# Another order of work between the down product and the output gate of a two-block transformer layer

## The chip, the cores and the metric

The kernel runs on one core of one Trainium2 chip. Its time is the device time of one execution in microseconds. The profile comes from one profiled execution; in it, TensorE (PE) does the matmuls and transposes, ScalarE (ACT), VectorE (DVE) and GpSimd (POOL) do the rest, and SyncE (SP) starts the DMA transfers of the weights.

## The reference

Two blocks run one after the other on x of 512 rows and 1024 columns, all in fp32. The first is a mixed attention layer, the second an attention and convolution layer with a feed-forward part and, at the very end, an input gate. What the change touches is the end of the second block:

```python
f = (jax.nn.silu(h @ w_gate[i]) * (h @ w_up[i])) @ w_down[i]   # down product, 2816 -> 1024
x = x + rmsnorm(f, ffn_post_norm[i])
e = rmsnorm(p[i] @ w_ple_proj[i], ple_norm[i])
x = x + jax.nn.sigmoid(x @ w_ple_gate[i]) * e                  # the gate, 1024 -> 1024
```

`rmsnorm(x, g)` is x / sqrt(mean(x^2) + 1e-6) * g over a row.

## The kernel before

**Precision.** Every operand of a product is kept as a high half and a low half (what the high half leaves over), and every product is three matmuls: high x high, high x low, low x high. Weights come in 142 chunks of 128 x 1024 through two raw buffers; ScalarE or GpSimd makes a chunk's high half (`w_hi`), GpSimd its low half (`w_lo`, two instructions of 128 x 512). There are four slots for split chunks, chunk c in slot c mod 4, and a slot is free again when the last matmul on its chunk has counted up `w_used`. For the down product ScalarE makes the high halves of the weights; for the gate GpSimd makes both.

**Rows.** The 512 rows stand in T = 4 row tiles of 128, called rows 0 to 3 here. The activations of the down product (`act`, 22 tiles of 128 x 512, k = 0..21) are staged one by one: ScalarE copies the high half into `aT_hi` (`stage` at line 1547), VectorE takes the low half (`stage` at line 2105), and TensorE waits for `staged`.

**The down product** (lines 1078 to 1122). `down_step(t, k)` is the six matmuls of row t with chunk k (two halves of 512 columns, three matmuls each). Up to k = 18 each chunk is used for all four rows (`down_block`, 24 matmuls); the last three chunks are used row by row, so that row 0 ends first. Row t fills PSUM banks 2t and 2t+1.

**What follows a row of it.** ScalarE squares the two banks with a row sum, VectorE adds the two sums (line 2134) and makes the mean (1636), ScalarE does logarithm and exponential (1205, 1206), VectorE three small Newton steps (1643 to 1648), then two scaled products (1631) and the addition to x (2009, counts up `x_new`). TensorE turns the new row of x with eight transposes into two tiles called xT (`turn_x`), ScalarE copies the high halves (`turned_hi`), VectorE takes the low halves (`turned_lo`, line 1663). `x_row(t)` is TensorE's wait for row t's halves.

**The gate** (lines 1125 to 1178). `pgate_step(g, t, n)` is the six matmuls of row t with chunk n of column half g; four chunks make a half. The first half runs mostly row by row, with the turns of rows 1 to 3 between: each turn has one to three steps of an earlier row behind it, before that row's halves are waited for. The second half takes chunks 0 and 1 for all rows, then chunks 2 and 3 row by row; its last row tile is done in two pieces of 256 columns. Sigmoid, product with `emb`, addition and store follow for each finished tile (lines 1607 to 1611 and 2143 to 2148).

**Order.** Every engine's instructions are written out by hand and run in that order; between engines there are only semaphores. `psum_tiles` (line 71) lists the PSUM tiles in the order in which they take their banks, each with the engine that empties it; from it come the counts that TensorE waits for.

## Time and profile before

| | |
|---|---|
| time, median of 3 runs | 946.56 us (944.69 to 948.07) |
| profiled execution | 944.69 us |
| its span on the core | 943.0 us |
| TensorE busy | 926.2 us (98%) |
| VectorE busy | 392.5 us (42%) |
| ScalarE busy | 331.2 us (35%) |
| GpSimd busy | 474.1 us (50%) |
| mean granted clock of TensorE | 0.994 |

The span runs from the first to the last instruction of the core; the profiled execution's own time is 1.7 us longer. The stage that the change touches is about the last 80 us: the block of k = 18 runs from 867 us, the rows of the down product after it to about 889 us, the first half of the gate to 916 us, the second to 939 us. In a stream, a matmul's duration is longer than the distance to the next one's start, since they are pipelined: the distances are what counts.

### The profile page before, as it was taken

What the parts mean: (1) busy time and instruction counts of PE and PEld (TensorE: products, weight loads), DVE (VectorE), ACT (ScalarE), POOL (GpSimd) and SP (SyncE); (2) the same over time, 40 slices, a digit from 0 to 9 for tenths busy, and PEclk for the clock granted to TensorE, in tenths of its full rate; (3) what the DMA queues carried; (4) which work ended last, traced back from release to release, by engine and by line L of the source; (5) the groups of instructions that cost most, each with busy time, mean ns of one, the idle gap of its engine ahead of it and who ended that gap; (6) DMA issues with size and microseconds to landing.
All of it is one profiled execution on the core that took longest, in us unless ns stands there. A gap on an engine that the chain in (4) does not pass through costs nothing.

```text
span 943.0 us, 12707 instructions
## 1 busy us (share of the span) xinstructions
PE 926.2 (98%) x4548; PEld 748.7 (79%) x4548; DVE 392.5 (42%) x647; ACT 331.2 (35%) x661; POOL 474.1 (50%) x376
## 2 busy tenths in 40 slices
PE   8999999999999999999999999999999999999998
PEld 7889877665578988886767988888888888888787
DVE  1654454557413283595648551111111122222662
ACT  3333414455312402175645842222222232323321
POOL 7967673230046776780334474454454445555543
PEclk9999999998999999999999999999999999999999
DMA  6432321100012332221111332322322322322213
GB/s 216 130 109 91 112 91 67 45 24 23 1 37 96 96 112 93 104 90 46 45 45 46 112 112 89 111 89 91 110 89 91 132 89 90 111 90 89 68 64 115
DMA packets 28058, 81.55 MB, mean 86 GB/s; under 512 B 5984, under 2 KB 8416, under 8 KB 28016
## 3 DMA queue, kind: packets, MB, share of 16 engines
q1 hardware_dynamic: 23856, 78.65, 25.1%
q10 hardware_dynamic: 4160, 2.32, 0.9%
q8 instruction: 29, 0.48, 0.2%
q14 instruction: 13, 0.11, 0.0%
HBM read 78.83 MB, written 2.10 MB: 86 GB/s over the span
## 4 chain that ended last, share of the span: by engine, by line
PE 90%; DVE 5%; issue 2%; POOL 1%; ACT 1%; DMA 1%; SPq 0%; DVEq 0%; POOLq 0%; ACTq 0%
PE bank L471 25%; PE bank L473 25%; PE bank L472 25%; PE bank L663 4%; PE bank L528 3%; PE bank L744 2%; PE bank L686 2%; PE bank L734 1%; PE bank L757 1%; POOL w_lo L429 1%; DVE aT_lo L1631 1%; DVE x L2009 1%; DMA raw<-in_weights 1%; DVE arena L1631 1%; DVE PT L1974 0%
## 5 line engine op out<-in xcount | busy, mean ns | idle before, releaser
L429 POOL TENSOR_TENSOR w_lo<-raw,w_hi 128x512 fp32r<-128x512 f32 x282 | 386.5, 1392 | 202.1 <-ACT w_hi L1199 196.1
L471 PE MATMUL bank<-w_hi,aT_hi 128*128 128x512 f32 (+4 forms) x600 | 227.3, 379 | 6.2 <-POOL w_lo L429 4.1
L471 PE MATMUL bank<-aT_hi,w_hi 128*128 128x512 f32 (+1 forms) x600 | 230.5, 384 | 0.0
L473 PE MATMUL bank<-aT_hi,w_lo 128*128 128x512 f32 (+1 forms) x600 | 227.1, 378 | 0.0
L472 PE MATMUL bank<-aT_lo,w_hi 128*128 128x512 f32 (+1 forms) x600 | 226.9, 378 | 0.0
L473 PE MATMUL bank<-w_hi,aT_lo 128*128 128x512 f32 (+4 forms) x600 | 222.1, 370 | 0.0
L472 PE MATMUL bank<-w_lo,aT_hi 128*128 128x512 f32 (+4 forms) x600 | 221.9, 370 | 0.0
L422 POOL TENSOR_SCALAR w_hi<-raw 128x1024 fp32r<-128x1024 f32 x73 | 80.6, 1104 | 246.8 <-PE bank L473 213.1
L1199 ACT ACTIVATE w_hi<-raw 128x1024 fp32r<-128x1024 f32 x68 | 72.1, 1062 | 233.4 <-PE bank L473 220.6
L471 PEld LDWEIGHTS bank<-w_hi,aT_hi 128*128 128x128 f32 x600 | 113.0, 188 | 26.1 <-POOL w_lo L429 6.7
L473 PEld LDWEIGHTS bank<-aT_hi,w_lo 128*128 128x128 f32 x600 | 112.9, 188 | 21.0
L471 PEld LDWEIGHTS bank<-aT_hi,w_hi 128*128 128x128 f32 x600 | 113.0, 188 | 20.0 <-issue 0.5
L472 PEld LDWEIGHTS bank<-aT_lo,w_hi 128*128 128x128 f32 x600 | 113.1, 188 | 19.8 <-issue 0.2
L473 PEld LDWEIGHTS bank<-w_hi,aT_lo 128*128 128x128 f32 x600 | 112.9, 188 | 19.1
L472 PEld LDWEIGHTS bank<-w_lo,aT_hi 128*128 128x128 f32 x600 | 113.1, 189 | 16.6
L2107 DVE TENSOR_TENSOR aT_lo<-arena,aT_hi 128x512 fp32r<-128x512 f32 x22 | 27.3, 1249 | 78.0 <-ACT aT_hi L1199 78.0
L2096 DVE TENSOR_TENSOR arena<-arena,bank 128x512 f32 (+1 forms) x22 | 15.1, 687 | 94.6 <-PE bank L473 93.7
L2093 DVE TENSOR_TENSOR arena<-bank,R 128x512 f32<-128x512 f32 x22 | 15.2, 691 | 89.3 <-PE bank L473 89.2
L1331 ACT ACTIVATE h<-bank,negmax 128x128 f32<-128x128 f32 (+1 forms) x64 | 33.8, 529 | 49.1 <-DVE negmax L1796 48.7
L1796 DVE TENSOR_REDUCE negmax<-bank 128x1 f32<-128x128 f32 (+1 forms) x64 | 31.2, 489 | 40.7 <-PE bank L665 39.4
L663 PE MATMUL bank<-arena 66*128 66x128 f32 (+7 forms) x128 | 45.7, 438 | 0.8 <-DVE arena L1695 0.8
L1199 ACT ACTIVATE arena<-bank,stat 128x512 f32<-128x512 f32 (+3 forms) x32 | 19.6, 612 | 44.5 <-PE bank L473 40.9
(202 smaller groups left out, 850.9 us busy)
## 6 DMA issues: line engine op xcount, KB each, us to landing
raw<-in_weights SPq DMA_DIRECT2D x142, 512.0 KB, 3.3
x<-in_x SPq DMA_DIRECT2D x4, 512.0 KB, 7.6
y_out<-x SPq DMA_DIRECT2D x7, 256.0 KB, 4.1
g_post<-in_gains ACTq DMA_DIRECT2D x3, 512.0 KB, 3.3
arena<-in_pt ACTq DMA_DIRECT2D x1, 512.0 KB, 3.8
y_out<-x SPq DMA_DIRECT2D x2, 128.0 KB, 1.9
wpool<-in_wpool ACTq DMA_DIRECT2D x1, 128.0 KB, 5.7
g_col<-in_gains ACTq DMA_DIRECT2D x3, 4.0 KB, 4.3
```

The source lines that it names most:

```text
L422: nc.gpsimd.tensor_scalar(w_hi[:, s, :], raw[:, r, :], 1.0, 1.0, ALU.mult, ALU.mult).then_inc(hi_made, 1)
L429: lo = nc.gpsimd.tensor_tensor(w_lo[:, s, at], raw[:, r, at], w_hi[:, s, at].bitcast(F32), ALU.subtract)
L471: mm(out, st_hi, mv_hi, start=start, stop=False)
L472: mm(out, st_hi, mv_lo, start=False, stop=False)
L473: return mm(out, st_lo, mv_hi, start=False, stop=stop)
L528: return nc.tensor.transpose(out, in_, ident[:, :])
L663: mm(out[:, 0:kw], qT_[0:width, i, qb * P:(qb + 1) * P], kT_[0:width, i, 0:kw], start=True, stop=False)
L686: last = mm(bank[6][r0:r0 + HD, kb * P:S], v_[:, kb, i * HD:(i + 1) * HD], pt_of[i % 3][:, kb, kb * P:S], start=(kb == 0), stop=(kb == T - 1),
L1199: return A(out, in_, ACT.Copy, scale=scale)
L1331: A(P_buf[:, n % 4, 0:kw], bank[n % 3][:, 0:kw], ACT.Exp, bias=negmax[:, n % 8:n % 8 + 1], accum_out=esum[:, n % 8:n % 8 + 1]).then_inc(ex ...
L1796: V.tensor_reduce(negmax[:, n % 8:n % 8 + 1], bank[n % 3][:, 0:kw], AX_X, ALU.max, negate=True)\
L2107: V.tensor_tensor(aT_lo[:, slot, :].unsqueeze(1), act[:, bass.ds(k, 1), :], aT_hi[:, slot, :].bitcast(F32).unsqueeze(1), ALU.subtract).the ...
```

## The change

It rewrites the order of this last stage on four engines; no matmul is added or dropped.

- TensorE: the last four chunks of the down product, not three, are used row by row. Row 0 is turned after row 2 of the down product, row 1 inside row 3 ahead of its last two chunks, row 2 behind row 3. Then gate chunks 0 and 1 run for rows 0 to 2; then row 3 is turned and does chunks 0 and 1; then chunks 2 and 3 run for all rows. The second half of the gate runs row by row over all four chunks.
- ScalarE: in the down product, the copy of activation k comes just ahead of the weights of chunk k+3, no longer one further ahead; the last three copies (k = 19, 20, 21) all stand behind the last weights (chunk 21). The high halves of rows 0 and 1 stand ahead of row 3's squares, those of rows 2 and 3 behind row 3's square root.
- VectorE: the low halves of rows 0 and 1 stand ahead of row 3's sum, row 2's ahead of row 3's scaled products; none stands between scaled products and addition any more. The release of a down tile's banks counts after the addition.
- The table of PSUM tiles follows the new order: turned tiles 0 to 3 take banks 0 to 3, the others banks 4 to 7.

```diff
@@ psum_tiles
     for t in range(T):
-        if t == T - 1:
-            for n in range(2):
+        for g in range(2):
+            tiles["down", t, g] = (2 * t + g, "dve" if t < T - 1 else "dve_last",
+                                   CH["down"] + NF - 1 if (t, g) == (T - 1, 1) else None)
+        if t == T - 2:
+            for n in range(4):
                 tiles["xT", n] = (n, "dve", None)
...
@@ tensor
-            for k in range(4 * rounds, NF - 3):
+            for k in range(4 * rounds, NF - 4):
                 down_block(k, k % 4)
...
             for t in range(T):
-                if t == T - 1:
-                    turn_x(range(1))
-                for k in range(NF - 3, NF):
+                for k in range(NF - 4, NF):
                     if t == 0:
                         pe.wait_ge(staged, k + 1)
                         pe.wait_ge(w_split, k + CH["down"] + 1)
+                    if t == T - 1 and k == NF - 2:
+                        turn_x(range(1, 2))
                     down_step(t, k % 4, end=(k == NF - 1))
+                if t == T - 2:
+                    turn_x(range(0, 1))
...
-            def gate_row(t, ns):
-                for n in ns:
+            turn_x(range(2, T - 1))
+            for n in range(2):
+                for t in range(T - 1):
+                    if n == 0:
+                        x_row(t)
+                    pgate_step(0, t, n)
+            turn_x(range(T - 1, T))
+            x_row(T - 1)
+            for n in range(2):
+                pgate_step(0, T - 1, n).then_inc(w_used, 1)
+            for n in range(2, 4):
+                for t in range(T):
                     last = pgate_step(0, t, n)
                     if t == T - 1:
                         last.then_inc(w_used, 1)
                     elif n == 3:
                         last.then_inc(tile_full, 1)
-
-            x_row(0)
-            gate_row(0, (0,))
-            turn_x(range(1, 2))
-            gate_row(0, (1, 2))
-            x_row(1)
-            gate_row(1, (0, 1))
-            turn_x(range(2, 3))
-            gate_row(0, (3,))
-            gate_row(1, (2, 3))
-            x_row(2)
-            gate_row(2, (0,))
-            turn_x(range(3, 4))
-            gate_row(2, (1, 2, 3))
-            x_row(T - 1)
-            gate_row(T - 1, range(4))
-
-            halves = ((slice(0, S // 2), ("pgate", 1, T - 1)), (slice(S // 2, S), ("pgate", 2, T - 1)))
-            for n in range(2):
-                for t in range(T - 1):
-                    pgate_step(1, t, n)
-                pgate_step(1, T - 1, n, *halves[0])
-                pgate_step(1, T - 1, n, *halves[1]).then_inc(w_used, 1)
...
+            for n in range(3):
+                pgate_step(1, 0, n)
+            pgate_step(1, 0, 3).then_inc(tile_full, 1)
+            for t in range(1, T - 1):
+                for n in range(4):
+                    last = pgate_step(1, t, n)
+                last.then_inc(tile_full, 1)
+            for n in range(4):
+                last = pgate_step(1, T - 1, n, slice(0, S // 2))
+            last.then_inc(tile_full, 1)
+            for n in range(4):
+                pgate_step(1, T - 1, n, slice(S // 2, S), ("pgate", 2, T - 1)).then_inc(w_used, 1)
@@ scalar
-            stage(4, 0, CH["down"] + 1)
             rounds = (NF - 4) // 4
             with act_.Fori(1, rounds) as i:
                 for j in range(4):
-                    stage(i * 4 + (j + 1), (j + 1) % 4, i * 4 + (CH["down"] + j - 2))
+                    stage(i * 4 + j, j, i * 4 + (CH["down"] + j - 3))
                     down_weights(i * 4 + j, j)
             for k in range(4 * rounds, NF - 3):
-                stage(k + 1, (k + 1) % 4, CH["down"] + k - 2)
-                if k == NF - 4:
-                    stage(k + 2, (k + 2) % 4, CH["down"] + k - 1)
+                stage(k, k % 4, CH["down"] + k - 3)
                 down_weights(k, k % 4)
-            stage(NF - 1, (NF - 1) % 4, CH["down"] + NF - 4)
+            for k in range(NF - 3, NF):
+                stage(k, k % 4, CH["down"] + k - 3)
...
             for t in range(T):
-                if t == T - 2:
-                    turned_hi("xT", range(1))
+                if t == T - 1:
+                    turned_hi("xT", range(0, 2))
                 for g in range(2):
                     full(act_, ("down", t, g))
                     squares(tbank(("down", t, g))[:, :], 16 + 2 * t + g, stat[:, 3, 12 + t:13 + t])
-                if t == T - 1:
-                    turned_hi("xT", range(1, 2))
                 rsqrt(slice(24 + t, 25 + t))
@@ vector
             for t in range(T):
+                if t == T - 1:
+                    turned_lo("xT", range(0, 2))
                 sqn[0] += 2
                 dve.wait_ge(sq_done, sqn[0])
...
                 newton(24 + t, stat[:, 3, 12 + t:13 + t])
-                add_post(t, [(g * 512, (g + 1) * 512, tbank(("down", t, g))[:, :]) for g in range(2)], 24 + t,
-                         lambda: down_read(t))
+                if t == T - 1:
+                    turned_lo("xT", range(2, T - 1))
+                add_post(t, [(g * 512, (g + 1) * 512, tbank(("down", t, g))[:, :]) for g in range(2)], 24 + t)
+                for g in range(2):
+                    if t < T - 1:
+                        order[0] += 1
+                    V.sem_inc(drained[tiles["down", t, g][3][0]], 1)
```

The numbers of lines in the rows below are each kernel's own; those of the changed kernel are 2 to 14 lower for the same statement.

ScalarE at the end of the down product, before: the copies `aT_hi<-arena` are activations 17; 18; 19 and 20; 21, and the `w_hi<-raw` between them are chunks 19, 20 and 21.

```order
L1199 ACTIVATE aT_hi<-arena 128x512 [waits w_used]
L1199 ACTIVATE w_hi<-raw 128x1024 [waits w_used,raw_in1]
L1199 ACTIVATE aT_hi<-arena 128x512 [waits w_used]
L1199 ACTIVATE w_hi<-raw 128x1024 [waits w_used,raw_in0]
L1199 ACTIVATE aT_hi<-arena 128x512 [waits w_used] x2
L1199 ACTIVATE w_hi<-raw 128x1024 [waits w_used,raw_in1]
L1199 ACTIVATE aT_hi<-arena 128x512 [waits w_used]
```

The same place in the changed kernel; the copies are activations 16; 17; 18; then 19, 20 and 21.

```order
L1191 ACTIVATE aT_hi<-arena 128x512 [waits w_used]
L1191 ACTIVATE w_hi<-raw 128x1024 [waits w_used,raw_in1]
L1191 ACTIVATE aT_hi<-arena 128x512 [waits w_used]
L1191 ACTIVATE w_hi<-raw 128x1024 [waits w_used,raw_in0]
L1191 ACTIVATE aT_hi<-arena 128x512 [waits w_used]
L1191 ACTIVATE w_hi<-raw 128x1024 [waits w_used,raw_in1]
L1191 ACTIVATE aT_hi<-arena 128x512 [waits w_used] x3
```

Activations 19 and 20 moved from ahead of the last weights to behind them.

TensorE at the turn of row 3 (`ident,x` are its transposes), before:

```order
L528 MATMUL bank<-ident,x 128x128 [waits drained_dve_last,x_new]
L528 MATMUL bank<-ident,x 128x128 x3
L528 MATMUL bank<-ident,x 128x128 [waits drained_dve_last]
L528 MATMUL bank<-ident,x 128x128 x3
L471 MATMUL bank<-w_hi,aT_hi 128x512 [waits w_split]
```

And in the changed kernel:

```order
L526 MATMUL bank<-ident,x 128x128 [waits drained_dve_last,x_new]
L526 MATMUL bank<-ident,x 128x128 x3
L526 MATMUL bank<-ident,x 128x128 [waits drained_dve_last]
L526 MATMUL bank<-ident,x 128x128 x3
L469 MATMUL bank<-w_hi,aT_hi 128x512 [waits drained_dve,w_split,mix_lo]
```

The matmul behind the turn was one of row 2, which waits for a chunk alone; now it is row 3's own first, which waits for the low halves (`mix_lo`).

VectorE from row 3's sum on, in the changed kernel; the four low halves ahead of the sum are those of rows 0 and 1, the two behind the Newton steps those of row 2:

```order
L1651 TENSOR_TENSOR aT_lo<-bank,aT_hi 128x4x128 [waits mix_hi]
L1651 TENSOR_TENSOR aT_lo<-bank,aT_hi 128x4x128 [waits mix_lo,mix_hi] x3
L2116 TENSOR_TENSOR stat<-stat 128x1 [waits mix_lo,sq_done]
L1624 TENSOR_SCALAR stat<-stat 128x1 [waits dve_step]
L1631 TENSOR_SCALAR stat<-stat 128x1 [waits rs_made]
L1632 TENSOR_SCALAR stat<-stat 128x1 [waits dve_step]
L1636 TENSOR_SCALAR stat<-stat 128x1 [waits dve_step]
L1651 TENSOR_TENSOR aT_lo<-bank,aT_hi 128x4x128 [waits mix_hi,dve_step]
L1651 TENSOR_TENSOR aT_lo<-bank,aT_hi 128x4x128 [waits mix_lo,mix_hi]
L1619 SCALAR_TENSOR_TENSOR PT<-bank,stat,g_post 128x512 [waits mix_lo]
```

Before, row 3's sum came straight after the addition of row 2, and row 2's low halves between row 3's scaled products and its addition.

```order
L2009 TENSOR_TENSOR x<-x,PT 128x1024 [waits mix_lo]
L2134 TENSOR_TENSOR stat<-stat 128x1 [waits sq_done]
L1636 TENSOR_SCALAR stat<-stat 128x1 [waits dve_step]
L1643 TENSOR_SCALAR stat<-stat 128x1 [waits rs_made]
L1644 TENSOR_SCALAR stat<-stat 128x1 [waits dve_step]
L1648 TENSOR_SCALAR stat<-stat 128x1 [waits dve_step]
L1631 SCALAR_TENSOR_TENSOR PT<-bank,stat,g_post 128x512 [waits dve_step] x2
L1663 TENSOR_TENSOR aT_lo<-bank,aT_hi 128x4x128 [waits dve_step,mix_hi]
L1663 TENSOR_TENSOR aT_lo<-bank,aT_hi 128x4x128 [waits mix_lo,mix_hi]
L2009 TENSOR_TENSOR x<-x,PT 128x1024 [waits mix_lo]
```

So row 2's low halves moved ahead of the scaled products, and those of rows 0 and 1 came to stand between row 2's addition and row 3's sum.

## Rows read from the trace of the kernel before

**Rows 1.** The page: TensorE's share of the span; the chain by engine.
```profile
PE 926.2 (98%) x4548; PEld 748.7 (79%) x4548; DVE 392.5 (42%) x647; ACT 331.2 (35%) x661; POOL 474.1 (50%) x376
...
PE 90%; DVE 5%; issue 2%; POOL 1%; ACT 1%; DMA 1%; SPq 0%; DVEq 0%; POOLq 0%; ACTq 0%
```

**Rows 2.** Waits of TensorE, 600 us to the end: sum, times, longest.
```profile
PE bank L471 <- POOL w_lo L429: 2.3, 2, 2.0
```

**Rows 3.** TensorE by time: start, duration (us), line, operation, count, idle before.
```profile
866.99 0.39 PE L471 MATMUL bank<-w_hi,aT_hi 128*128 128x512 f32 x1
...
868.35 0.39 PE L471 MATMUL bank<-w_hi,aT_hi 128*128 128x512 f32 x1
...
893.10 0.39 PE L473 MATMUL bank<-w_hi,aT_lo 128*128 128x512 f32 x1
895.44 0.50 PE L471 MATMUL bank<-w_hi,aT_hi 128*128 128x512 f32 x1 [1.95 <-POOL w_lo L429]
...
905.99 1.03 PE L528 MATMUL bank<-ident,x 128*128 128x128 f32 x8
906.78 0.47 PE L471 MATMUL bank<-w_hi,aT_hi 128*128 128x512 f32 x1
...
916.19 0.39 PE L473 MATMUL bank<-w_hi,aT_lo 128*128 128x512 f32 x1
916.91 0.50 PE L471 MATMUL bank<-w_hi,aT_hi 128*128 128x512 f32 x1 [0.33 <-POOL w_lo L429]
...
939.07 0.28 PE L473 MATMUL bank<-w_hi,aT_lo 128*128 128x256 f32 x1
```

**Rows 4.** ScalarE by time, last weights' and last activations' high halves.
```profile
867.25 1.06 ACT L1199 ACTIVATE w_hi<-raw 128x1024 fp32r<-128x1024 f32 x1 [3.34 <-PE bank L473]
868.21 0.61 ACT L1199 ACTIVATE aT_hi<-arena 128x512 fp32r<-128x512 f32 x1
```

**Rows 5.** VectorE by time, low halves of the activations.
```profile
863.53 2.96 DVE L2107 TENSOR_TENSOR aT_lo<-arena,aT_hi 128x512 fp32r<-128x512 f32 x2 [4.18 <-ACT aT_hi L1199]
868.86 1.37 DVE L2107 TENSOR_TENSOR aT_lo<-arena,aT_hi 128x512 fp32r<-128x512 f32 x1 [2.37 <-ACT aT_hi L1199]
```

**Rows 6.** GpSimd by time, high and low halves of gate chunks 0 and 4.
```profile
872.78 1.05 POOL L422 TENSOR_SCALAR w_hi<-raw 128x1024 fp32r<-128x1024 f32 x1 [1.40 <-issue]
873.91 2.53 POOL L429 TENSOR_TENSOR w_lo<-raw,w_hi 128x512 fp32r<-128x512 f32 x2
...
912.68 1.24 POOL L422 TENSOR_SCALAR w_hi<-raw 128x1024 fp32r<-128x1024 f32 x1 [12.70 <-PE bank L473]
914.01 2.85 POOL L429 TENSOR_TENSOR w_lo<-raw,w_hi 128x512 fp32r<-128x512 f32 x2
```

**Rows 7.** VectorE by time, row 0's sum, last Newton step, addition to x.
```profile
877.78 0.16 DVE L2134 TENSOR_TENSOR stat<-stat 128x1 f32<-128x1 f32 x1 [7.55 <-ACT PT L1213]
...
879.34 0.27 DVE L1648 TENSOR_SCALAR stat<-stat 128x1 f32<-128x1 f32 x1
...
881.43 1.23 DVE L2009 TENSOR_TENSOR x<-x,PT 128x1024 f32<-128x1024 f32 x1 [0.25 <-DVE PT L1631]
```

**Rows 8.** VectorE by time, row 1's addition, row 2's sum, row 3's low halves.
```profile
887.69 1.70 DVE L2009 TENSOR_TENSOR x<-x,PT 128x1024 f32<-128x1024 f32 x1
889.31 1.25 DVE L2134 TENSOR_TENSOR stat<-stat 128x1 f32<-128x1 f32 x1
...
907.26 1.53 DVE L1663 TENSOR_TENSOR aT_lo<-bank,aT_hi 128x512 fp32r<-128x512 f32 x2 [2.32 <-ACT aT_hi L1199]
```

**Rows 9.** ScalarE by time, row 3's high halves and the last sigmoid.
```profile
906.63 1.09 ACT L1199 ACTIVATE aT_hi<-bank 128x512 fp32r<-128x512 f32 x2 [5.25 <-PE bank L528]
...
939.38 0.38 ACT L1611 ACTIVATE PT<-bank 128x256 f32<-128x256 f32 x1 [1.05 <-DVE x L2148]
```

**Rows 10.** Windows: busy us of PE, PEld, DVE, ACT, POOL; granted clock, DMA share, GB/s.
```profile
220.00:225.00 5.00, 5.00 (x11) 2.51 (x11) 4.92 (x9) 2.73 (x6) 0.00 (x0) 0.50 0.00 0
...
892.00:900.00 8.00, 6.05 (x29) 4.66 (x29) 6.78 (x11) 2.14 (x6) 7.74 (x6) 1.00 0.39 131
```

More of the change, by code:

```diff
@@ L152, in psum_tiles @@
     for t in range(T):
-        if t == T - 1:
-            for n in range(2):
+        for g in range(2):
[3 more added lines that the diff above has]
+            for n in range(4):
                 tiles["xT", n] = (n, "dve", None)
-        for g in range(2):
-            tiles["down", t, g] = (2 * t + g, "dve_last", CH["down"] + NF - 1 if (t, g) == (T - 1, 1) else None)
-    for n in range(2, 6):
+    for n in range(4, 2 * T):
         tiles["xT", n] = (n, "dve", None)
     for t in range(T):
-        if t == 2:
-            for n in range(6, 2 * T):
-                tiles["xT", n] = (n, "dve", None)
         tiles["pgate", 0, t] = (t, "act", CH["pgate"] + 3 if t == T - 1 else None)
@@ L1148, in gate_row @@
                         last.then_inc(tile_full, 1)
-            x_row(0)
-            gate_row(0, (0,))
-            turn_x(range(1, 2))
-            gate_row(0, (1, 2))
-            x_row(1)
-            gate_row(1, (0, 1))
-            turn_x(range(2, 3))
-            gate_row(0, (3,))
-            gate_row(1, (2, 3))
-            x_row(2)
-            gate_row(2, (0,))
-            turn_x(range(3, 4))
-            gate_row(2, (1, 2, 3))
-            x_row(T - 1)
-            gate_row(T - 1, range(4))
-            halves = ((slice(0, S // 2), ("pgate", 1, T - 1)), (slice(S // 2, S), ("pgate", 2, T - 1)))
-            for n in range(2):
-                for t in range(T - 1):
-                    pgate_step(1, t, n)
-                pgate_step(1, T - 1, n, *halves[0])
-                pgate_step(1, T - 1, n, *halves[1]).then_inc(w_used, 1)
-            for t in range(T - 1):
-                pgate_step(1, t, 2)
-                pgate_step(1, t, 3).then_inc(tile_full, 1)
-            pgate_step(1, T - 1, 2, *halves[0])
-            pgate_step(1, T - 1, 3, *halves[0]).then_inc(tile_full, 1)
-            for n in (2, 3):
-                pgate_step(1, T - 1, n, *halves[1]).then_inc(w_used, 1)
+            for n in range(3):
[10 more added lines that the diff above has]
+                pgate_step(1, T - 1, n, slice(S // 2, S), ("pgate", 2, T - 1)).then_inc(w_used, 1)
         @block.scalar
@@ L1999, in _, with add_post @@
             V.sem_inc(sqs_made, 1)
-            def add_post(t, halves, at, between=None):
+            def add_post(t, halves, at):
                 for n, (lo_c, hi_c, value) in enumerate(halves):
@@ L2005, in add_post @@
                     own(stt(w, value, stat[:, 3, at:at + 1], g_post[:, lo_c:hi_c], ALU.mult, ALU.mult))
-                if between:
-                    between()
                 xn[0] += 1
@@ L2124, in _ @@
             dve.wait_ge(g_post_in, 48)
-            def down_read(t):
-                for g in range(2):
-                    V.sem_inc(drained["dve_last"], 1)
-                if t > 0:
-                    turned_lo("xT", range(t - 1, t))
             for t in range(T):
+                if t == T - 1:
+                    turned_lo("xT", range(0, 2))
                 sqn[0] += 2
```

## Prediction

> **What bounds the kernel now.** I read the page's busy shares and its chain by engine first. TensorE is busy for 926.2 of 943.0 us, and 90% of the chain that ended last is TensorE [rows 1]. So the time is TensorE's fixed work plus its pauses. The diff touches only the last 80 us or so. There I went to the waits of that window, then to TensorE's instructions in order of time, then to ScalarE, VectorE and GpSimd beside them.
>
> Between 860 us and the end TensorE pauses twice, both times for a low half made by GpSimd, 2.3 us in all [rows 2]. In a steady stream a 512-column matmul starts 0.227 us after the one before (the rows at 866.99 and 868.35 are six apart) [rows 3]. Counted from start to start, the first pause is 895.44 - 893.10 - 0.23 = 2.1 us and the second 916.91 - 916.19 - 0.23 = 0.5 us; the first matmul after a pause costs 0.1 more than the pitch, in every pause. This is the only time in the stage that another order could win back: **2.6 us**. The other waits of TensorE there are hidden by matmuls that stand between a turn and the row that needs it.
>
> **The change, part by part.** The matmuls are the same in number and size, and so are the four pairs of turned tiles. A step here is the six matmuls of one chunk for one row, 6 x 0.227 = 1.36 us; a row of the gate or of the down product over four chunks is four steps, 5.44 us; two turned tiles with the restart cost 906.78 - 905.99 + 0.1 = 0.9 us [rows 3]. What changes is who is ready when.
>
> **(a) Staging of the last four chunks of the activations.** The block of all rows for k=17 ends at 866.99, where before had another whole block (k=18) to run, to 866.99 + 24 x 0.227 = 872.43. Now row 0 of k=18..21 begins there, and k=19 is wanted after one step, at 868.35 [rows 3]. But ScalarE now copies the high half of k=19 only behind the weights of chunk 21, and these wait for the end of the block of k=17: in the trace they start at 867.25, and a copy behind them at 868.21 [rows 4]. VectorE's low half follows at 868.86; it took 1.37 alone and 2.96 for two in a row, about 1.48 each, beside GpSimd's splits [rows 5]. So k=19 is ready between 868.86 + 1.25 and + 1.48, about 870.3: a pause of 1.95 and 0.1 for the restart. k=20 and k=21 come 1.48 apart, against steps of 1.36: 0.1 to 0.2 more. **2.2 us**, bounds 1.9 and 2.4. In the loop before it the same delay is harmless: the low half is done 3 us into a block of 5.44. Row 0 then ends at 874.65, row 2 at 885.55, row 3 with both turns at 892.75.
>
> **(b) GpSimd and the gate's chunks.** Gate chunk 0 takes the slot of down chunk 18, which now is free only after row 3's first step, 887.8; GpSimd starts 0.3 later, as at 872.78 behind the block that ended at 872.43, and a chunk takes 3.6 (1.05 + 2.53) to 4.5 us [rows 6]. So chunk 0 is there at 891.8 to 893.1, chunk 1 at 895.5 to 897, chunks 2 and 3 by about 905. They are wanted at 893.6, about 900 and 910: no pause, and the 2.1 us of before go, because the order now does two chunks for three rows before it needs the third. The splits are only later, and that puts them beside VectorE's row chain, which counts in (c).
>
> **(c) Row 2 of the new order.** TensorE turns row 2 at 892.75, does step (row 0, chunk 0), (row 1, chunk 0), and wants row 2's halves at 892.75 + 0.9 + 2 x 1.36 = 896.4. VectorE's queue before these halves is: row 2's addition to x, four low halves of rows 0 and 1, row 3's sum of squares, its mean and Newton steps. The unhindered chain, from row 0 of before: the row ends at 876.5, the sum starts at 877.78, the Newton steps end at 879.61 = 1.83 later, the addition ends at 882.66, 6.15 after the row's end [rows 7]. So row 2 (end 885.55) has its new x at 891.7. The four low halves take 2 x 1.53 [rows 8]: VectorE is free at 894.9. The squares of row 3 are done at 892.75 + 1.27 = 894.0 and don't decide. From the sum on: 1.83 + 1.53 = 3.4. ScalarE's high halves of row 2, now behind row 3's square root, start with its end, 0.8 before the Newton steps do, and take 1.1 [rows 9]; they are hidden. Without any hindrance row 2 is ready at 898.3: a pause of 1.9 + 0.1.
>
> There is a hindrance. The sum took 0.16 us in the free chain, but 1.25 at 889.31, while GpSimd was making a low half, and the 128x1024 addition took 1.23 alone but 1.70 beside it [rows 7, 8]. In the changed kernel GpSimd splits chunk 0 and chunk 1 from 888.1 on, over this very addition and sum. If both are hit as in those rows, row 2 is ready 1.1 + 0.5 later, and with 0.3 more if the sum has to let a second low half through, a pause of 3.9; if VectorE is free as soon as the squares are (894.0) and nothing hits, 1.2. I take 2.7, one hit of two: **2.7 us**, bounds 1.2 and 3.9. The Trainium skill ("SBUF — State Buffer", section "SBUF: two separate sides") says that VectorE with two SBUF inputs and GpSimd exclude each other for a whole instruction. By that rule the pause would lie between 2.0 and 3.9, by how many of the two meet a split; without it, it would be 2.0. The trace agrees with it in the 1.25 against 0.16.
>
> **(d) Row 3 of the new order.** Row 3's turn and its first use now stand next to each other: three steps of row 2 stood between. From turn to low half in the trace: 905.99 to 907.26 + 1.53 = 908.79, with ScalarE and VectorE idle before [rows 3, 8, 9]. Of these 2.8 us the turn itself covers 0.8, and 0.1 is the switch that is paid anyway. Row 3's x is ready by about 903, before TensorE comes to turn it at 904.5. **2.1 us**, bounds 2.0 and 2.2 (TensorE's own rows give no other price for it).
>
> **(e) The second half of the gate.** Its first row now takes all four chunks in a row, and its chunk 3 sits in a slot that the very last step of the first half frees. That step is three steps, 4.1 us, ahead of the use. GpSimd started 912.68, 0.34 after such a step, and took 4.2 us beside VectorE's output products (2.85 + 1.24 + a gap), 3.7 without [rows 6]. So it is ready 4.0 to 5.0 after the step: 0 to 0.9, and since VectorE still has the first half's four outputs to do at that time, **0.5 us**. It stands where the 0.5 of before stood.
>
> **(f) The end.** The last half tile ends in product, addition and store as before. Before, the last sigmoid's row names VectorE's addition of the tile before as its releaser, which would be a gain now that this tile is done 2.9 us earlier; but it starts at 939.38, only 0.03 after the last matmul's end (939.07 + 0.28), so at most 0.03 is to be had [rows 3, 9]. Steps of down that gave up the turn before row 3 and took it back as two: 0. Later notice of the free down banks: VectorE's count now comes after the addition, but the turn waits for that addition anyway: 0.
>
> **The sum**: 2.2 + 2.7 + 2.1 + 0.5 - 2.6 = **+4.9 us**. On the profiled execution (944.69 us, of which 943.0 span and 1.7 around it) that is 949.6; this execution was the fastest of the three shown, 1.9 under their median, and a median of the changed kernel should stand to 946.56 as this stands to that: **951.5 us**. The bounds of all terms together are +2.5 and +6.8, that is 949.1 to 953.4.
>
> **The rivals.** About 0.3%, 2.8 us, is what a measurement of this kernel can tell from no change.
>
> - *VectorE has caught up (not slower by what can be told).* Place: row 2's halves. If the addition and the sum slip through between GpSimd's instructions, and row 3's squares decide, (c) is 1.2; if chunk 3 then is in time too, the sum is 2.2 + 1.2 + 2.1 - 2.6 = +2.9, and with (a) at 1.9, +2.6: 949.2. It decides from (c) below 1.1 with (e) at zero. For it: both instructions are short against GpSimd's gaps. Against it: GpSimd has no gap while two splits are pending. Chance 0.13, and 0.03 more that something I took for fixed gives time back and it is faster.
> - *The clock falls.* Three pauses of 2 to 3 us within 40 us are new. In this trace TensorE's granted clock is 1.00 from 892 to 900 us, around the 2.1 us pause, but between 220 and 225 us, with 11 matmuls in 5 us, it was 0.50, the lower of its two levels (1.2 of 2.4 GHz) [rows 10]. That stretch lost 5 x 0.5 = 2.5 us. The same here would give +7.4: 954.0. Against it: dense 512-column matmuls stand around each pause, and the clock held in the like case. Chance 0.07. The Trainium skill ("TensorE: Matmul & The Clock Gate", Part 1) has the half clock as the state an idle engine goes back to; this trace agrees only for the sparse stretch.
> - *The staging pause isn't there*, because the copies slip ahead somewhere I misread: +2.7, 949.3. ScalarE runs its queue in order and the waits are in its rows, so 0.04; it is part of the 0.13.
>
> **How the numbers follow.** The forecast, with (a) to (e) in their bounds and the clock at its full level, has 0.77; the clock 0.07; the catching up 0.13; faster 0.03. The forecast's low corner, below +2.8, is in the 0.13. So slower 0.84, same 0.13, faster 0.03. The range: the bounds 949.1 to 953.4, widened by about a microsecond below and one and a half above for medians of a kernel whose three runs spread over 3.4 us, and for the clock's case: 948.2 to 955.0.
>
> **What would show it.** In the changed trace: a pause of about 2 us in row 0 of the last down chunks, released by VectorE's low half of the activations (a); no pause for gate chunks 1 and 2 (b); a pause of 1.2 to 3.9 released by VectorE's low half of x about 4 us after the turn of row 2, and VectorE's sum ahead of it at over 1 us if the hindrance is real (c); a pause of 2.1 right behind the turn of row 3 (d); at most 0.9 for GpSimd three steps into the second half (e). I am wrong if (a) or (d) is missing, if a pause appears in the loop before 866 us, or if the clock leaves 1.00 there.

## The result and the profile after

The changed kernel took 951.05 us, the median of 13 executions (947.97 to 954.84), against 946.56 us before, also of 13. The medians differ by 4.5 us; the ratio on record, which is not simply the quotient of these medians, is 1.0054 with a 95% interval of 1.0039 to 1.007, that is 5.1 us more (3.7 to 6.6). The prediction was 951.5 us, and slower.

The two profiled executions are further apart than that, 951.42 us against 944.69, and part of this lies ahead of the change. ScalarE starts on the weights of chunk 21, 0.26 us behind the end of the block of k = 17, at 869.44 us instead of 867.25 [rows 4], 2.19 us later, though TensorE has no wait between 600 and 866 us in either trace. Most of it arose where TensorE's work is sparse: the same ScalarE instruction starts 0.31 us later in the changed kernel at about 208 us (208.75 against 208.44) and 2.16 us later at about 296 us (297.22 against 295.06). The windows from 200 to 300 us (columns as in [rows 10]), first of the kernel before, then of the changed kernel:

```profile
200.00:300.00 100.00, 98.36 (x417) 65.85 (x412) 41.48 (x85) 31.94 (x75) 22.22 (x19) 0.95 0.10 32
```

```profile
200.00:300.00 100.00, 98.36 (x406) 64.92 (x403) 40.93 (x84) 32.14 (x77) 22.11 (x18) 0.93 0.10 32
```

The granted clock was 0.95 of full speed in one and 0.93 in the other. So in what follows the **stage**, the stretch that the change touches, is measured by itself: from ScalarE's start on the weights of chunk 21 to the start of the last matmul. It was 939.07 - 867.25 = 71.82 us before and is 945.80 - 869.44 = 76.36 us after: **4.54 us more**, against +4.9 predicted.

TensorE's waits in the stage, as in [rows 2]: sum, times, longest.

```profile
PE bank L469 <- DVE aT_lo L1651: 3.5, 2, 1.8
PE bank L469 <- DVE aT_lo L2093: 1.7, 1, 1.7
PE bank L469 <- POOL w_lo L427: 0.8, 1, 0.8
```

Before there were two waits for GpSimd's low halves of weights, 2.3 us. Now there are three for VectorE, 5.2 us, and one for GpSimd. The same in TensorE's order of time (the answer to [rows 3]):

```profile
870.32 0.39 PE L471 MATMUL bank<-w_hi,aT_lo 128*128 128x512 f32 x1
872.45 0.51 PE L469 MATMUL bank<-w_hi,aT_hi 128*128 128x512 f32 x1 [1.74 <-DVE aT_lo L2093]
...
887.88 1.03 PE L526 MATMUL bank<-ident,x 128*128 128x128 f32 x8
...
895.12 1.03 PE L526 MATMUL bank<-ident,x 128*128 128x128 f32 x8
...
898.52 0.39 PE L471 MATMUL bank<-w_hi,aT_lo 128*128 128x512 f32 x1
900.63 0.50 PE L469 MATMUL bank<-w_hi,aT_hi 128*128 128x512 f32 x1 [1.72 <-DVE aT_lo L1651]
...
906.21 1.03 PE L526 MATMUL bank<-ident,x 128*128 128x128 f32 x8
...
909.06 0.50 PE L469 MATMUL bank<-w_hi,aT_hi 128*128 128x512 f32 x1 [1.81 <-DVE aT_lo L1651]
...
926.65 0.39 PE L471 MATMUL bank<-w_hi,aT_lo 128*128 128x512 f32 x1
927.80 0.50 PE L469 MATMUL bank<-w_hi,aT_hi 128*128 128x512 f32 x1 [0.76 <-POOL w_lo L427]
...
945.80 0.28 PE L471 MATMUL bank<-w_hi,aT_lo 128*128 128x256 f32 x1
```

The pause at 872.45 is row 0 waiting for activation k = 19, the one at 900.63 is row 2 of the gate, the one at 909.06 is row 3 right behind its turn (906.21), the one at 927.80 the last weight chunk of the second half. ScalarE and VectorE around the first (the answer to [rows 4, 5]):

```profile
869.44 1.06 ACT L1191 ACTIVATE w_hi<-raw 128x1024 fp32r<-128x1024 f32 x1 [3.86 <-PE bank L471]
870.41 1.65 ACT L1191 ACTIVATE aT_hi<-arena 128x512 fp32r<-128x512 f32 x3
```

```profile
871.16 3.53 DVE L2093 TENSOR_TENSOR aT_lo<-arena,aT_hi 128x512 fp32r<-128x512 f32 x3 [4.18 <-ACT aT_hi L1191]
...
892.31 1.67 DVE L1995 TENSOR_TENSOR x<-x,PT 128x1024 f32<-128x1024 f32 x1
893.90 3.19 DVE L1651 TENSOR_TENSOR aT_lo<-bank,aT_hi 128x512 fp32r<-128x512 f32 x4
897.24 0.31 DVE L2116 TENSOR_TENSOR stat<-stat 128x1 f32<-128x1 f32 x1
...
899.05 1.53 DVE L1651 TENSOR_TENSOR aT_lo<-bank,aT_hi 128x512 fp32r<-128x512 f32 x2
```

The copies of 19, 20 and 21 stand in one piece behind the weights, and VectorE's three low halves behind them. The other rows of VectorE are row 2's addition to x, the four low halves of rows 0 and 1, row 3's sum and row 2's low halves (the answer to [rows 7, 8]). GpSimd beside them (the answer to [rows 6]): high and low halves of gate chunk 0, then the low halves of chunk 1.

```profile
890.48 1.05 POOL L420 TENSOR_SCALAR w_hi<-raw 128x1024 fp32r<-128x1024 f32 x1 [16.94 <-issue]
891.61 3.53 POOL L427 TENSOR_TENSOR w_lo<-raw,w_hi 128x512 fp32r<-128x512 f32 x2
...
896.24 2.54 POOL L427 TENSOR_TENSOR w_lo<-raw,w_hi 128x512 fp32r<-128x512 f32 x2
```

### The profile page after: what moved, and what is told of

Read it like the earlier page. It is cut to its first block, busy times and chain, and to the rows that moved or that the text cites. A ratio compares the mean times of both kernels' runs of the same rounds, so it can differ in the third digit from the quotient of the medians.

```text
span 949.7 us, 12711 instructions
## 1 busy us (share of the span) xinstructions
PE 928.8 (98%) x4548; PEld 749.2 (79%) x4548; DVE 389.8 (41%) x647; ACT 331.4 (35%) x661; POOL 474.6 (50%) x376
## 4 chain that ended last, share of the span: by engine, by line
PE 90%; DVE 6%; ACT 1%; issue 1%; DMA 1%; POOL 1%; POOLq 0%; DVEq 0%; SPq 0%; ACTq 0%
PE bank L469 25%; PE bank L471 25%; PE bank L470 25%; PE bank L661 4%; PE bank L526 3%; PE bank L742 2%; PE bank L684 2%; PE bank L732 1%; PE bank L755 1%; DVE aT_lo L1619 1%; DVE x L1995 1%; DVE aT_lo L1651 1%; DVE PT L1619 1%; DMA raw<-in_weights 1%; DVE arena L1619 1%
```

## The experiments

Each was run beside the kernel before on the same chip; "stage" is the length defined above, in one profiled execution each.

| run | median, us (executions) | ratio to before, 95% interval | stage, us |
|---|---|---|---|
| kernel before, beside the changed kernel | 946.56 (13) | | 71.82 |
| changed kernel | 951.05 (13) | 1.0054 (1.0039 to 1.007) | 76.36 |
| e1, copies ahead | 949.09 (10) | 1.0046 (1.0029 to 1.0063) | 74.56 |
| e2, row 2 later | 948.5 (10) | 1.0042 (1.0021 to 1.0062) | 74.57 |
| e3, row 3 covered | 953.2 (5) | 1.009 (1.0056 to 1.0123) | 80.21 |
| e4, second half | 949.61 (10) | 1.005 (1.0032 to 1.0069) | 76.98 |
| e5, all four | 942.78 (12) | 0.998 (0.9966 to 0.9994) | 69.66 |
| e6, before with late copies | 944.19 (10) | 0.9985 (0.9969 to 1.0002) | 71.81 |
| e7, short low halves | 951.82 (1) | | 77.01 |
| e8, short splits | 949.36 (1) | | 74.73 |
| e9, changed again | 951.29 (4) | 1.0061 (1.0038 to 1.0083) | 78.25 |
| e10, changed a third time | 946.42 (1) | | 76.53 |
| e11, all four again | 944.41 (12) | 0.9984 (0.9968 to 1.0) | 69.63 |

The kernel before had medians of 945.05 beside e1 to e4, 945.28 beside e5 to e7 and 945.2 beside e8 to e11. The ratios are those on record and differ a little from the quotients of the medians (0.9974 for e5). The totals are too close together to part single terms of 1 to 2 us (the intervals are 2.6 us wide or more); the stage is what tells them apart.

### e1: the copies ahead again

```diff
+            stage(4, 0, CH["down"] + 1)
...
-                    stage(i * 4 + j, j, i * 4 + (CH["down"] + j - 3))
+                    stage(i * 4 + (j + 1), (j + 1) % 4, i * 4 + (CH["down"] + j - 2))
                     down_weights(i * 4 + j, j)
...
-            for k in range(NF - 3, NF):
-                stage(k, k % 4, CH["down"] + k - 3)
+            stage(NF - 1, (NF - 1) % 4, CH["down"] + NF - 4)
```

> The changed kernel with ScalarE's order of activation copies as in the kernel before (one further ahead, 19 and 20 ahead of the weights of chunk 21); all else as changed. Theory: late copies alone make the pause in row 0 of the last down chunks; it goes, and since everything behind it depends on row ends, nothing takes its place. The stage, from ScalarE's start on the weights of chunk 21 to the start of the last matmul, was 76.36 us in the changed kernel and 71.82 before; it should be 74.0, the total about 2.4 us (0.25%) under the changed kernel. Rival: the pause only hides that the row chain behind it is late, and a pause of like size comes back at row 1's or row 2's turn: stage 76.0 or more.

The stage fell by 1.80 us, and nothing came back at the later rows. But it did not fall by the whole 2.4, so it ended at 74.56 and not at the expected 74.0. TensorE in row 0, changed kernel with copies ahead:

```profile
872.54 0.39 PE L471 MATMUL bank<-w_hi,aT_lo 128*128 128x512 f32 x1
873.22 0.47 PE L469 MATMUL bank<-w_hi,aT_hi 128*128 128x512 f32 x1 [0.29 <-POOL w_lo L427]
```

The wait moved from k = 19 to k = 21, and its releaser from VectorE's activations to GpSimd's low half of the weights of chunk 21. These can't start before the block of k = 17 has ended, in either order. So of the 2.4 us, 1.8 belong to the late copies and 0.6 to starting row-by-row work one chunk earlier; of these 0.6, this wait is 873.22 - 872.54 - 0.23 = 0.45.

### e2: row 2 after four steps

```diff
-            for n in range(2):
-                for t in range(T - 1):
-                    if n == 0:
-                        x_row(t)
-                    pgate_step(0, t, n)
+            for t in range(2):
+                x_row(t)
+                pgate_step(0, t, 0)
+            for t in range(2):
+                pgate_step(0, t, 1)
+            x_row(2)
+            for n in range(2):
+                pgate_step(0, 2, n)
```

> The changed kernel with four steps instead of two between row 2's turn and row 2's first step: rows 0 and 1 do gate chunks 0 and 1 before row 2 starts. Theory: the pause of 1.9 us before row 2 is VectorE's queue (low halves of rows 0 and 1, row 3's statistics, then row 2's halves) against a cover of two steps; two more steps of 1.36 cover it. Gate chunk 1 is ready at about the time it is wanted. Stage 76.4 - 1.9 = 74.5. Rival: GpSimd's chunk 1 takes the place of the wait, as chunk 2 does in the kernel before: a pause of 0.5 to 2 for a low half of weights, stage 75 to 76.4.

The stage fell by 1.79, and TensorE's waits in it are those of the changed kernel less one:

```profile
PE bank L469 <- DVE aT_lo L1654: 1.8, 1, 1.8
PE bank L469 <- DVE aT_lo L2096: 1.7, 1, 1.7
PE bank L469 <- POOL w_lo L427: 0.7, 1, 0.7
```

The pause before row 2 is gone and chunk 1 did not take its place. The theory held.

### e3: two steps behind row 3's turn

```diff
             turn_x(range(T - 1, T))
+            for t in range(2):
+                pgate_step(0, t, 2)
             x_row(T - 1)
...
             for n in range(2, 4):
-                for t in range(T):
+                for t in range(2 if n == 2 else 0, T):
```

> The changed kernel with two steps (rows 0 and 1, gate chunk 2) between row 3's turn and row 3's first step. Theory: the 2.05 us behind row 3's turn are the bare way from turn to low half and any two steps cover them; chunk 2 is split 4 us earlier. Stage 76.4 - 2.05 = 74.3. Rival: chunk 2 isn't there, or the second half's chunks 4 and 5, whose slots row 3 frees two steps later than before, come late: stage 75 to 77.

The pause behind the turn went, as expected, and the stage still grew by 3.85 us. The rival is what happened, and more, though at other chunks than it named: chunks 6 and 7, not 4 and 5. GpSimd, the high halves of chunks 4 to 7 of the gate and the last low half:

```profile
909.49 1.05 POOL L420 TENSOR_SCALAR w_hi<-raw 128x1024 fp32r<-128x1024 f32 x1 [4.51 <-PE bank L471]
...
913.12 1.05 POOL L420 TENSOR_SCALAR w_hi<-raw 128x1024 fp32r<-128x1024 f32 x1
...
917.22 1.50 POOL L420 TENSOR_SCALAR w_hi<-raw 128x1024 fp32r<-128x1024 f32 x1
...
922.05 1.49 POOL L420 TENSOR_SCALAR w_hi<-raw 128x1024 fp32r<-128x1024 f32 x1
923.63 3.25 POOL L427 TENSOR_TENSOR w_lo<-raw,w_hi 128x512 fp32r<-128x512 f32 x2
```

All four splits of the second half now stand end to end; in the changed kernel the first three did, and the fourth began after a gap of 0.85 us (the row at 923.15 under (e) below). The first starts 5.3 us behind row 3's turn (909.49 - 904.15) instead of 4.7 (910.90 - 906.21), because row 3 frees chunk 0 two steps later, while the pause that is gone lets the second half begin 2.1 us sooner. TensorE waits first for chunk 6 (0.61 us idle before the matmul at 922.14), then for chunk 7, whose split ends at 926.88:

```profile
923.40 0.40 PE L471 MATMUL bank<-w_hi,aT_lo 128*128 128x512 f32 x1
926.93 0.79 PE L469 MATMUL bank<-w_hi,aT_hi 128*128 128x512 f32 x1 [3.13 <-POOL w_lo L427]
927.52 0.63 PE L470 MATMUL bank<-w_lo,aT_hi 128*128 128x512 f32 x1
927.95 0.63 PE L471 MATMUL bank<-w_hi,aT_lo 128*128 128x512 f32 x1
```

After 3.13 us of pause the matmuls come 0.43 us apart instead of 0.23: the granted clock was 0.57 from 925 to 930 us and 0.74 from 930 to 935. From this pause to the end took 947.58 - 926.93 = 20.65 us, against 945.80 - 927.80 = 18.00 us in the changed kernel for the same work. The pause cost 926.93 - 923.40 - 0.23 = 3.30 us and the clock another 2.65. Together: -2.06 for the pause that is gone, +0.76 for chunk 6, 3.30 - 0.92 = +2.38 for chunk 7 and +2.65 for the clock are +3.7, of 3.85 measured.

### e4: the second half in its old order

```diff
-            for n in range(3):
-                pgate_step(1, 0, n)
-            pgate_step(1, 0, 3).then_inc(tile_full, 1)
...
+            for n in range(2):
+                for t in range(T - 1):
+                    pgate_step(1, t, n)
+                pgate_step(1, T - 1, n, *halves[0])
+                pgate_step(1, T - 1, n, *halves[1]).then_inc(w_used, 1)
...
```

> The changed kernel with the second half of the gate in the order of the kernel before (chunks 0 and 1 for all rows, then 2 and 3 row by row); the first half as changed. Theory: the pause of 0.8 to 0.9 us three steps into the second half is the split of its last chunk; in this order that chunk is wanted 8 steps or more later, and the pause of 0.5 that the kernel before had at the start of its second half doesn't return, because the first half's order as changed frees slots 0 and 1 early. Stage 76.4 - 0.9 = 75.5. Rival: the pause only moves to another chunk: 76.4.

The pause went and did not move:

```profile
PE bank L469 <- DVE aT_lo L1652: 3.5, 2, 1.8
PE bank L469 <- DVE aT_lo L2094: 1.7, 1, 1.7
```

Yet the stage was 0.62 longer, not 0.9 shorter. Behind row 3's turn, in a stretch that this edit doesn't touch, TensorE ran

```profile
908.61 0.50 PE L469 MATMUL bank<-w_hi,aT_hi 128*128 128x512 f32 x1 [1.81 <-DVE aT_lo L1652]
...
909.98 0.63 PE L471 MATMUL bank<-w_hi,aT_lo 128*128 128x512 f32 x1
910.41 0.63 PE L469 MATMUL bank<-w_hi,aT_hi 128*128 128x512 f32 x1
```

at 0.43 us a matmul from 909.98 on, for 3.3 us. That is the lower level of the clock (granted 0.50 in the window from 910 to 913 us), behind a pause that is the same in the changed kernel (1.81 us idle). 76.98 less the expected 75.5 is 1.5 us. The expectation was wrong in total and right in the term it was made for; the clock is taken up in e9.

### e5 and e11: all four edits

The edits of e1 to e4 together, in one kernel.

> The changed kernel with all four edits at once (copies ahead, row 2 after four steps, two steps behind row 3's turn, second half in the order of before). Theory: the four pauses are independent, and with the two early pauses for weights gone that the change does remove, TensorE has no pause over 0.3 us left in the stage: 76.36 - 2.38 - 1.9 - 2.05 - 0.87 = 69.2 us, 2.6 under the kernel before, total about 0.27% faster than before. Rival: the pauses cover each other (VectorE and GpSimd used them to catch up), and a new one of 1 to 2 us appears at gate chunk 1 or 2: stage 70.5 to 71.5, no measurable gain on before.

The stage was 69.66 us, and TensorE's waits in it

```profile
PE bank L469 <- POOL w_lo L427: 0.3, 1, 0.3
```

are the 0.3 us for chunk 21 seen in e1. Counted from start to start this wait is 0.45, and 71.82 - 2.6 + 0.45 = 69.67. The expected 69.2 had missed it: it took off the whole 2.4 of row 0, where moving the copies wins back only 1.8. What failed by itself in e3 works here: the four splits stand end to end here too (they start at 904.29, 907.93, 912.03 and 916.87), but with the second half in the old order chunk 7 is wanted late enough. The total was 0.2% under the kernel before, 0.998 (0.9966 to 0.9994). A second time:

> The kernel with all four edits once more, for its interval against the kernel before. Theory: no pause over 0.3 us behind the down product, so no fall of the clock in the stage: stage 69.7, total 0.2% to 0.3% under the kernel before. Rival: the first gain was chance of the mean clock: no difference.

69.63 us, and 0.9984 (0.9968 to 1.0). The stage repeats to 0.03 us; 71.8 - 69.65 = 2.2 us, 0.23%, agrees with both ratios. The second interval reaches 1.0, so that the gain in total rests on the first and on the stage.

### e6: late copies in the kernel before

The kernel before with ScalarE's part of the change alone (the diff of e1 turned round).

> The kernel before with ScalarE's order of activation copies as changed (19, 20 and 21 behind the weights of chunk 21); all else as before. Theory: late copies cost only together with row-by-row work that starts at k=18; here a block of all four rows at k=18 (5.4 us) stands between and hides them: stage 71.8 as before, no difference in total. Rival: late copies cost by themselves, somewhere in the loop or at k=19: stage 73 to 74.

Stage 71.81 us, and the two waits of before, to a tenth:

```profile
PE bank L471 <- POOL w_lo L429: 2.3, 2, 2.0
```

Late copies cost nothing while a block of four rows stands between. They cost 1.8 us once row-by-row work begins a chunk earlier: neither edit is expensive alone.

### e7 and e8: GpSimd out of VectorE's way

```diff
-                    at = slice(half * 512, (half + 1) * 512)
+                    at = slice(half * 512, half * 512 + width)
...
+            for c in range(CH["pgate"], NCH):
+                split(c, c % SLOTS, False, skipped=CH["pgate"] - SHARED, width=32)
```

> The changed kernel with GpSimd's low halves of the eight gate chunks made for 32 of each 512 columns only, so that part of the low halves of the gate's weights is left out; it takes GpSimd's long instructions away from beside VectorE's row chain. Theory (VectorE with two operands in SBUF waits for GpSimd's instruction): row 2's addition falls from 1.67 to 1.23 us and row 3's sum from 0.31 to 0.16, the pause before row 2 from 1.9 to 1.3, and the pause for the last chunk of the second half goes (0.9): stage 76.4 - 0.6 - 0.9 = 74.9. Rival (GpSimd has no hand in the pause before row 2): that pause stays at 1.9, stage 75.5.

The pause before row 2 stayed at 1.9 us, which was the rival's number, but the run doesn't decide: row 2's addition was not set free. (The stage of 77.01 lacks the pause for the last chunk, as expected, and has instead the fall of the clock that e9 is about.) VectorE's addition and the GpSimd instruction that it now met, gate chunk 1's high half:

```profile
891.99 1.85 DVE L1996 TENSOR_TENSOR x<-x,PT 128x1024 f32<-128x1024 f32 x1
```

```profile
891.73 1.05 POOL L420 TENSOR_SCALAR w_hi<-raw 128x1024 fp32r<-128x1024 f32 x1
```

1.85 us, against 1.23 alone. So e8 leaves out most of the high halves of the gate's weights too:

```diff
-                    nc.gpsimd.tensor_scalar(w_hi[:, s, :], raw[:, r, :], 1.0, 1.0, ALU.mult,
+                    hw = slice(0, CW if width == 512 else 32)
+                    nc.gpsimd.tensor_scalar(w_hi[:, s, hw], raw[:, r, hw], 1.0, 1.0, ALU.mult,
```

> The changed kernel with both halves of the eight gate chunks made for 32 columns of 512 (low) and 32 of 1024 (high), so that most of the split of the gate's weights is left out and GpSimd is next to idle in the stage. With the low halves alone shortened, GpSimd's high half at 891.73 met row 2's addition instead (1.85 us), so the hindrance was not removed. Theory: now the addition takes 1.23, row 2's halves come 0.4 to 0.6 earlier against row 2's turn, and the pause before row 2 falls from 1.9 to 1.3 to 1.5. Rival: the addition is not what the low halves of rows 0 and 1 wait for, and the pause stays within 0.1 of 1.9.

VectorE's addition, the four low halves of rows 0 and 1 and row 3's sum, then TensorE at row 2:

```profile
891.80 1.23 DVE L1997 TENSOR_TENSOR x<-x,PT 128x1024 f32<-128x1024 f32 x1
892.94 3.20 DVE L1653 TENSOR_TENSOR aT_lo<-bank,aT_hi 128x512 fp32r<-128x512 f32 x4
896.29 0.16 DVE L2118 TENSOR_TENSOR stat<-stat 128x1 f32<-128x1 f32 x1
```

```profile
899.53 0.50 PE L471 MATMUL bank<-w_hi,aT_hi 128*128 128x512 f32 x1 [1.15 <-DVE aT_lo L1653]
```

The addition took 1.23 us and the sum 0.16. From row 2's turn (its place in the stage is 25.70) to row 2's first step (30.62) it took 4.92 us instead of 5.51: the pause is 1.3 instead of 1.9. The hindrance by GpSimd is worth 0.6 us (0.44 at the addition, 1.67 for 1.23, and 0.15 at the sum, 0.31 for 0.16); the rest of the pause is VectorE's queue itself. The addition and the sum have both operands in SBUF and were held up; the four low halves, with one operand in PSUM, took 3.19 us beside GpSimd's splits (893.90 in the changed kernel) and 3.20 without. Both agree with the rule of the Trainium skill ("SBUF — State Buffer", section "SBUF: two separate sides") that VectorE, when both its inputs are in SBUF, and a GpSimd instruction that reads SBUF exclude each other for a whole instruction.

### e9 and e10: the changed kernel again

> The changed kernel once more. Theory: its executions come in two kinds, by whether TensorE's granted clock falls to the lower level behind the pause at row 3's turn: stage 76.4 us without (as in the trace of the changed kernel), 77.9 with (as the two variants with the second half reordered and with short low halves showed). The times of all executions then follow the mean clock at about 900 us for each unit of it (0.9 us for 0.001). Rival: the fall belonged to those two variants alone, stage 76.4 always.

> The changed kernel a third time, for the same question: a stage of 76.4 us (clock 1.00 throughout) or of 77.9 (a fall behind the turn of row 3). If neither this nor the run before it shows 77.9, the fall is not shown for the changed kernel itself.

The stage was 78.25 us in e9 and 76.53 in e10, with the same pauses before and behind row 3's turn. The windows around the pause behind that turn, first e9 (pause until 907.24), then e10 (until 903.90):

```profile
905.00:910.00 5.00, 3.19 (x13) 2.39 (x12) 1.38 (x2) 2.37 (x3) 0.75 (x2) 0.83 0.34 108
910.00:915.00 5.00, 5.00 (x20) 4.02 (x19) 0.00 (x0) 0.00 (x0) 4.83 (x5) 0.83 0.13 32
```

```profile
900.00:905.00 5.00, 3.19 (x19) 2.53 (x18) 1.38 (x2) 2.37 (x3) 1.87 (x2) 1.00 0.34 107
905.00:910.00 5.00, 5.00 (x24) 4.14 (x23) 0.00 (x0) 0.00 (x0) 4.18 (x4) 1.00 0.01 3
```

0.83 twice against 1.00 twice: the same program, with and without the fall. The price can be read between two matmuls that are the same in all: from the restart behind the turn to the last matmul ahead of the next pause took 926.46 - 907.24 = 19.22 us in e9, against 17.58 in e10 and 926.65 - 909.06 = 17.59 in the first trace of the changed kernel, 1.6 us more. The rest of the 1.7 to 1.9 us between the stages is a longer wait for the last chunk (1.15 us in e9, 1.07 in e10, 0.92 in the first trace). Counting every trace with this pause behind the turn of row 3 (the changed kernel, e1, e2, e4, e7, e8, e9, e10), the clock fell there in three of eight: e4, e7, e9. It fell 1.0 to 1.4 us after the matmuls had begun again (in e4 they began at 908.61 and the pitch of 0.43 us at 909.98), not in the pause itself.

The expectation had a second part, and it was too simple: the mean clock of an execution orders the totals, but this is another matter than the fall behind the turn. The executions of the changed kernel run from 947.97 us at a mean clock of 0.996 to 954.84 at 0.989, 0.98 us for each 0.001, near the 0.9 expected. Yet the first trace and e9 took nearly the same time, 951.42 and 951.46 us, one without the fall and one with it: the windows from 200 to 300 us have a granted clock of 0.93 and 0.95 there, and of 0.98 in e10 with its 946.42 us. So in these two the sparse stretch far ahead of the change made up for the fall, and a total doesn't tell whether the fall was there. The spread of 3.4 us between the first three executions of before is of the size that such differences of the clock give.

## Why the prediction was right, point by point

Each pause that was forecast is there, at its place and with its releaser, and an edit aimed at each takes it away: e1 for (a), but for the 0.45 us of chunk 21, e2 for (c), e3 for (d), where others come in its place, and e4 for (e). That the number came out closer than its terms is luck: (a) is 0.2 too small, (e) 0.4 too small and (c) 0.8 too large.

| term | predicted, us (bounds) | measured, us | read from |
|---|---|---|---|
| early pauses gone | -2.6 | -2.6 | no wait for gate chunks 0 to 6 |
| (a) activation k = 19 | +2.2 (1.9 to 2.4) | +2.4 | 887.88 - 869.18 - 72 x 0.2267 |
| (c) row 2 | +2.7 (1.2 to 3.9) | +1.9 | 900.63 - 895.12 - 0.9 - 2 x 1.36 |
| (d) row 3 | +2.1 (2.0 to 2.2) | +2.06 | 909.06 - 906.21 - 0.79 |
| (e) last chunk | +0.5 (0 to 0.9) | +0.9 | 927.80 - 926.65 - 0.23 |
| sum | +4.9 | +4.7; stage +4.54 | |

(869.18 is the end of the block of k = 17: 869.44 less the 0.26 us between that end and ScalarE's start.)

**(a)** came out as worked out, at its upper bound: the copies start 0.97 us behind the weights, the first low half 1.72 behind them, where the trace of before had 0.96 and 1.61. What the step put down to the copies alone is, by e1, 1.8 us of theirs and 0.6 of the weights of chunk 21, which would have been the next wait. The step didn't ask what is late next once the copies are in time.

**(b)** held: chunks 0 to 3 of the gate were never waited for. GpSimd's first split began 2.6 us behind row 2's end, as computed, and ran into VectorE's row chain.

**(c)** is the term that was mis-sized, 2.7 for 1.9. Its mechanism was right: e2 takes the pause away with two more steps of cover, e8 shows GpSimd's share. The sizes were not. Without any hindrance the prediction had 2.0; e8 measures 1.3. Most of the difference is that I counted a free chain of 6.15 us from a row's end to its addition's end; with products and addition next to each other in VectorE's order now (no 0.25 us gap, [rows 7]) the addition began 0.5 earlier (4.4 us behind the row's end at 887.88, not 4.9). GpSimd then held it for 0.44 (1.67 for 1.23), so that the two nearly cancelled. And the sum, which could have been held for a full 1.1, met the very end of a low half: GpSimd's two instructions from 896.24 are 1.27 each, the first ends at 897.51, and the sum, started at 897.24, ended at 897.55. I had taken one hit of two, about 0.8; in fact both were touched, at 0.44 and 0.15. The sign that I had named for a real hindrance, a sum of over 1 us, did not show; that it is real rests on e8.

**(d)** came out within 0.05. But the recorded working doesn't lead to it as written: 2.8 less 0.8 for the turn and less 0.1 for the switch is 1.9, and only with the 0.1 added, as the cost of the restart, is it the 2.1 given. The 2.85 us from turn to first matmul (909.06 - 906.21) less the 0.79 of the turn is what was measured. It is the term with the least in it: an operation chain on idle engines, read off the trace of before.

**(e)** came out at its upper bound, 0.9. GpSimd's last split in the changed kernel:

```profile
923.15 1.22 POOL L420 TENSOR_SCALAR w_hi<-raw 128x1024 fp32r<-128x1024 f32 x1 [0.85 <-PE bank L471]
924.45 3.29 POOL L427 TENSOR_TENSOR w_lo<-raw,w_hi 128x512 fp32r<-128x512 f32 x2
```

It took 1.22 and 3.29 us beside VectorE's products, where I had 1.24 and 2.85 from [rows 6]. This row of the trace of before, the low halves of gate chunk 5, also beside VectorE, would have been the nearer one:

```profile
917.96 3.30 POOL L429 TENSOR_TENSOR w_lo<-raw,w_hi 128x512 fp32r<-128x512 f32 x2
```

The errors of (c) on one side and of (a) and (e) on the other have opposite signs, so the sum is nearer than its terms.

**(f)** held: the last sigmoid starts with the last matmul's end.

**The rivals.** VectorE did not catch up; with (c) at 1.9 it stood 0.8 above the 1.1 below which that rival decides. The clock's fall was given 0.07, with a price of 2.5 us. It is a real part of this kernel: shown in one of its three traces, at 1.6 us. My argument against it, that the clock held at the like pause of before, rested on one execution and one pause. The pause behind row 3's turn follows eight short transposes; the one before row 2, of 1.9 us between full matmuls, saw no fall in any trace. That this difference is the reason is argued, not shown. The measured total of 5.1 us (3.7 to 6.6) and the stage of 4.54 without a fall are compatible with a fall in some executions; how often it comes is not settled by three traces.

## What to carry to other kernels

When work is handed over row by row, count for every wait the steps between the turn and the first use of its result, and give each at least the length of the chain on idle engines (here 2.8 us, of which the turn covers 0.8 and two steps the rest), and more where an engine of the chain has other work ahead in its queue, as for row 2; then ask what becomes late next, since e1 and e3 both uncovered a wait behind the one they removed. Where the refills of shared slots stand end to end, look at when the last of them is first wanted: e3 lost 3.9 us, 2.65 of them to the clock, by a reordering that removes a pause of 2 us, while in e5, where the order of the second half gave its last chunk time, the same edit brought no such wait. Compare the stage, from a fixed instruction to a fixed instruction, when totals vary by more than the effect.

## What the hardware did that I had not expected

TensorE's granted clock fell to the lower level of 1.2 GHz behind a pause of 2.06 us that followed 0.8 us of 128x128 transposes, in some executions of a program and not in others (e9 and e10), for 3.3 us in e4 and at a price of 1.5 us in e4 and 1.6 in e9; in the kernel before it stayed at 1.00 through a pause of 2.1 us. After a pause of 3.30 us (e3) it cost 2.65 us. The Trainium skill ("TensorE: Matmul & The Clock Gate", Part 1) says that the chip's watch on TensorE runs freely and does not start with the kernel; that the same program shows both agrees with it.

A pause of TensorE can thus cost nearly twice its own length: 2.06 + 1.6 us in e9, 3.30 + 2.65 us in e3.
